# Hybrid decoder layer: the gates' columns in the first v pair, o slots four tiles wide, the mixer's first chunk among the last input slots

## The reference, cut to what matters

```
h    = rms_norm(x) * pre_mix_norm_w                # x: 2048 tokens x 1024
proj = h @ w_in      # columns: q, k (1024), v (512), o (512), gates (8), conv value (512), conv gate (512)
q, k = silu(causal depthwise conv, width 4, of their columns)
i, f = gates + gate_bias                           # 4 heads each
h_tilde = mLSTM(q, k, v, i, log_sigmoid(f))        # 16 chunks of 128 tokens, a state carried on
y_mlstm = sigmoid(o) * head_norm(h_tilde) * mlstm_norm_w
y_conv  = silu(group_norm(causal conv, width 31, of value * sigmoid(gate)))
x = x + rms_norm([y_mlstm, y_conv] @ w_out);  x = x + rms_norm(relu(rms_norm(x) @ w_ff1)^2 @ w_ff2)
```

## Time and profile before

| | |
|---|---|
| time, median of 3 runs | 2147.93 us (2145.79 to 2150.26) |
| the profiled execution | 2149.32 us, of which the span is 2147.5 us |
| PE | 2090.3 us busy, 97% of the span |
| DVE | 1441.8 us, 67% |
| ACT | 903.3 us, 42% |
| mean granted clock of PE | 0.994 of full |

### The profile page before, as it was taken

One profiled execution on the slowest core, in us unless ns is written; L12 is line 12 of the kernel. 1 busy time (PEld: TensorE's weight loads), 2 busy tenths in 40 slices (PEclk: granted clock), 3 DMA queues, 4 the chain that ended last, 5 costly groups with the idle time before them and its releaser, 6 DMA issues. The chain is left out here.

```text
span 2147.5 us, 27070 instructions
## 1 busy us (share of the span) xinstructions
PE 2090.3 (97%) x10177; PEld 1752.4 (82%) x10177; DVE 1441.8 (67%) x1965; ACT 903.3 (42%) x1512; POOL 416.3 (19%) x254
## 2 busy tenths in 40 slices
PE   7999999999979999999999999999999999999998
PEld 5897878888978888778888778888888888888886
DVE  6797999889157777776666866666654536534276
ACT  5532434234344544655544644455423313313153
POOL 0000000000010231243332332233172144400012
PEclk9999999999999999999999999999999999999999
DMA  5021212112174686664455655544875454443375
GB/s 198 25 89 47 67 40 84 55 40 81 55 271 154 223 270 222 210 199 141 139 159 181 227 161 162 162 147 125 280 253 222 142 230 172 175 176 138 137 253 207
DMA packets 253520, 339.18 MB, mean 158 GB/s; under 512 B 11536, under 2 KB 196112, under 8 KB 239568
## 3 DMA queue, kind: packets, MB, share of 16 engines
q1 hardware_dynamic: 219344, 316.29, 43.9%
q10 hardware_dynamic: 33728, 21.04, 3.1%
q0 software_dynamic: 320, 0.13, 0.0%
HBM read 226.14 MB, written 111.28 MB: 157 GB/s over the span
## 5 line engine op out<-in xcount | busy, mean ns | idle before, releaser
L1651 PE MATMUL psum<-x_hi,w_hi_P 128*128 128x512 f32 x896 | 351.6, 392 | 13.1 <-DVE x_lo L1595 8.9
L1855 PE MATMUL psum<-w_hi,hid_hi 128*128 128x512 f32 x896 | 349.3, 390 | 1.9 <-DVE hid_lo L1745 1.9
L1651 PE MATMUL psum<-x_hi,w_lo_P 128*128 128x512 f32 x896 | 350.4, 391 | 0.0
L1651 PE MATMUL psum<-x_lo,w_hi_P 128*128 128x512 f32 x896 | 350.2, 391 | 0.0
L1855 PE MATMUL psum<-w_lo,hid_hi 128*128 128x512 f32 x896 | 349.1, 390 | 0.0
L1855 PE MATMUL psum<-w_hi,hid_lo 128*128 128x512 f32 x896 | 349.1, 390 | 0.0
L1745 DVE TENSOR_TENSOR hid_lo<-hid_raw,hid_hi 128x1024 fp32r<-128x1024 f32 x112 | 182.1, 1663 | 202.4 <-ACT hid_hi L1740 202.4
L1564 POOL TENSOR_TENSOR w_raw<-w_raw 128x512 f32<-128x512 f32 x128 | 179.7, 1427 | 409.6 <-DVE w_lo_P L1577 391.6
L1740 ACT ACTIVATE hid_hi<-hid_raw 128x1024 fp32r<-128x1024 f32 x112 | 112.9, 1051 | 341.5 <-DMA hid_raw<-scratch_hid 341.5
L1577 DVE TENSOR_TENSOR w_lo_P<-w_raw,w_hi_P 128x512 fp32r<-128x512 f32 x224 | 182.4, 826 | 109.1 <-ACT w_hi_P L1573 106.0
L1573 ACT ACTIVATE w_hi_P<-w_raw 128x512 fp32r<-128x512 f32 x224 | 136.7, 627 | 255.0 <-PE psum L1651 254.8
(11 more groups left out here) (241 smaller groups left out, 3895.4 us busy)
## 6 DMA issues: line engine op xcount, KB each, us to landing
scratch_hid<-stage SPq DMA_DIRECT2D x224, 256.0 KB, 3.7
hid_raw<-scratch_hid SPq DMA_DIRECT2D x56, 1024.0 KB, 4.9
w_raw<-in_w SPq DMA_DIRECT2D x52, 1024.0 KB, 5.1
w_grain<-in_w SPq DMA_DIRECT2D x48, 512.0 KB, 4.9
x_raw<-scratch_h2s SPq DMA_DIRECT2D x14, 1024.0 KB, 7.5
w_raw<-in_w_in SPq DMA_DIRECT2D x25, 512.0 KB, 3.6
scratch_h2s<-h2s SPq DMA_DIRECT2D x8, 1280.0 KB, 9.2
scratch_qk<-qout ACTq DMA_DIRECT2D x16, 512.0 KB, 3.1
```

What stands on the lines that cost most here:

```text
L1651: mm = nc.tensor.matmul(psum[:, bank_1(op, g), :], l, r, start=kt == 0 and i == 0, stop=kt == 3 and i == 2)
L1855: mm = nc.tensor.matmul(psum[:, bank, :], l, r, start=f == 0 and k == 0, stop=f == NFP - 1 and k == 2)
```

## The change

- The 8 gate columns move into the weights of the first v pair. A slot of that pair streams 264 columns instead of 256, fills two banks, and begins when the first of its two weight tiles is split. ACT takes the gate columns out to a small tile (`gates`), token by token. PE turns it with two transposes (`gates_t`) after slot 73. The four gates slots, their tile, their stores and their loads go.
- Of the o slots the first six stay as they are (chunks 0 to 5); the other ten (`ow`) have 128 tokens held and four weight tiles streamed: 24 matmuls of 512. The list has 96 slots: o and ow are 80 to 95.
- The gates' row work is cut into four pieces, on DVE at the end of steps 76, 78, 80 and 82 (`forget_rows` to a_max, `carry_rows` to m_in, `floor_rows`, `column_rows`), on PE after slots 76, 78, 79 and 81 (`carry_in`, `carry_out`, `carry_decay`, `columns`), on ACT in steps 74, 78 and 80, each with two table loads.
- Banks go round four from slot 70 on and round two in the last five slots, 91 to 95.
- Chunk 0 runs among these: `scores(0)` after slot 91, `numerators(0)` after 92, `transpose_y(0)` and `scores(1)` after 94, with their work on ACT, DVE and POOL. It has buffers of its own for y.
- The last convolution unit's norm is drawn together (`LAST_UNIT_AT`): sums after slots 88 and 89, the rest in steps 88 and 89. `w_out` is loaded when slot 87 is done, and split in steps 92 to 95.

By the plan's own arithmetic over the new list, the last two convolution units end at steps 79 and 87; `SECOND_TAP` of the last one moves from step 78 to 79. On DVE the splits of tiles o0 and o1 stand in step 75, of o2 in 78, of o3 in 80.

```diff
+O_PAIRS = 3
 SLOTS = (group_slots(0) + pair_slots("v", 0) + group_slots(1) + group_slots(2) + pair_slots("v", 1) + group_slots(3)
-         + [("gates", 0, tb) for tb in range(NTB)] + pair_slots("o", 0) + pair_slots("o", 1))
+         + [("o", pair, m) for pair in range(2) for m in range(O_PAIRS)] + [("ow", 0, c) for c in range(2 * O_PAIRS, NCH)])
...
+RING = [0, 1, 2, 3] + [0, 1] + [2, 3, 0, 1] + [2, 3, 0, 1] + [2, 3] + [0, 1, 2, 3] + [0, 1, 2, 3]
+GATE_COLS = 2 * H
+VG = 2 * P + GATE_COLS
...
+ROWS_SLOT = SLOTS.index(("qk", 6, 0))
+CHUNK_0_SLOT = N_SLOTS - 5
+
+
+def banks_of(s):
+
+    if s >= CHUNK_0_SLOT:
+        return [(s - CHUNK_0_SLOT) % 2]
+    if s >= ROWS_SLOT - 2:
+        return [(s - ROWS_SLOT + 2) % 4]
+    at = s + sum(with_gates(slot) for slot in SLOTS[:s])
+    return [(at + k) % 6 for k in range(2 if with_gates(SLOTS[s]) else 1)]
...
+LAST_UNIT_AT = {AT_MEAN: 1, AT_CENTER: 1, AT_SQUARE: 1, AT_VAR: 2, AT_RSTD: 2, AT_NORM: 2, AT_SILU: 2}
...
-TAIL_SLOT = N_SLOTS - 6
+WO_SPLITS = {CHUNK_0_SLOT + 1: (0,), CHUNK_0_SLOT + 2: (1, 2, 3), CHUNK_0_SLOT + 3: (4,), CHUNK_0_SLOT + 4: (5, 6, 7)}
...
+                first = tile[0] if with_gates(SLOTS[s]) else tile[-1]
+                pe.wait_ge(sem["w_hi"], first + 1)
+                pe.wait_ge(sem["w_lo"], first + 1)
+                for bank in banks:
+                    before = last_in_bank(s, bank)
+                    if before is not None:
+                        by = "dve" if SLOTS[before][0] == "val" else "act"
+                        pe.wait_ge(sem["evac"][by], evacs(before, by))
                 r = RING[tile[0]]
...
+                if with_gates(SLOTS[s]):
+
+                    for k in range(2):
+                        o = psum[:, banks[k], 0:VG]
+                        for kt in range(KT):
+                            if k == 0 and kt == KT // 2:
+                                pe.wait_ge(sem["w_hi"], tile[1] + 1)
+                                pe.wait_ge(sem["w_lo"], tile[1] + 1)
+                            hi, lo = tokens(h_hi, kt, (2 * tb + k) * P, P), tokens(h_lo, kt, (2 * tb + k) * P, P)
+                            pairs = [(hi, vg_hi[:, kt]), (hi, vg_lo[:, kt]), (lo, vg_hi[:, kt])]
+                            for i, (a, b) in enumerate(pairs):
...
+                elif kind == "ow":
+
+                    o = out.rearrange("p (a b) -> p a b", a=W_RING)
+                    for kt in range(KT):
+                        hi, lo = tokens(h_hi, kt, tb * P, P), tokens(h_lo, kt, tb * P, P)
+                        pairs = [(hi, w_hi[:, :, kt, :]), (hi, w_lo[:, :, kt, :]), (lo, w_hi[:, :, kt, :])]
+                        for i, (a, b) in enumerate(pairs):
+                            mm = nc.tensor.matmul(o, a, b, start=kt == 0 and i == 0, stop=kt == KT - 1 and i == 2)
...
-                if s == TAIL_SLOT + 1:
+                if s == ROWS_SLOT + 1:
+                    pe.wait_ge(sem["evac"]["act"], evacs(ROWS_SLOT - 1, "act"))
+                    tail["gates"](pe)
+                if s == ROWS_SLOT + 4:
+                    tail["carry_in"](pe)
+                if s == ROWS_SLOT + 6:
+                    tail["carry_out"](pe)
+                if s == ROWS_SLOT + 7:
+                    tail["carry_decay"](pe)
+                if s == ROWS_SLOT + 9:
+                    tail["columns"](pe)
+                if s == CHUNK_0_SLOT:
                     pe.wait_ge(sem["c_rstd"], 2 * N_UNITS)
-                    tail["carry_in"](pe)
-                if s == TAIL_SLOT + 2:
-                    tail["carry_out"](pe)
-                if s == TAIL_SLOT + 3:
-                    tail["columns"](pe)
+                    scores(0)
+                if s == CHUNK_0_SLOT + 1:
+                    pe.wait_ge(sem["evac"]["act"], evacs(CHUNK_0_SLOT - 1, "act"))
+                    pe.wait_ge(sem["cols_done"], 2)
+                    numerators(0)
+                if s == CHUNK_0_SLOT + 3:
+                    transpose_y(0)
+                    scores(1)
...
+                    both = psum[:, banks[0]:banks[0] + 2, :]
+                    nc.scalar.activation(gates[:, :, :, 2 * tb:2 * tb + 2].rearrange("p g h c -> p c (g h)"),
+                                         both[:, :, 2 * P:VG], ACT.Copy)
+                    ps, to = both[:, :, 0:2 * P], to.rearrange("p (c d) -> p c d", c=2)
...
+                    if u == N_UNITS - 1:
+                        nc.scalar.preload_act_table_set(EXP_TANH)
...
-                if s == TAIL_SLOT:
+                if s == ROWS_SLOT + 2:
                     nc.scalar.preload_act_table_set(LN_EXP)
                     tail["softplus"](act)
                     nc.scalar.preload_act_table_set(SILU_TANH)
-                if s == TAIL_SLOT + 1:
+                if s == ROWS_SLOT + 6:
+                    nc.scalar.preload_act_table_set(LN_EXP)
+                    tail["decay"](act)
+                    nc.scalar.preload_act_table_set(SILU_TANH)
+                if s == ROWS_SLOT + 8:
                     nc.scalar.preload_act_table_set(LN_EXP)
                     tail["exps"](act)
                     nc.scalar.preload_act_table_set(SILU_TANH)
-                if s >= N_SLOTS - 3:
-
-                    if s == N_SLOTS - 1:
-                        nc.scalar.preload_act_table_set(LN_EXP)
-                        tail["weights"](act, 0)
-                    for kt in {N_SLOTS - 3: range(4), N_SLOTS - 2: range(4, 7), N_SLOTS - 1: ()}[s]:
-                        tail["split_wo"](act, kt)
+                if s == CHUNK_0_SLOT:
+                    act.wait_ge(sem["cols_done"], 2)
+                    tail["weights"](act, 0)
+                    first["wk"](0)
+                if s == CHUNK_0_SLOT + 1:
+                    first["yc_high"](0)
+                    nc.scalar.preload_act_table_set(LN_EXP)
+                    first["denominators"](0)
+                    first["head_roots"](0)
+                    nc.scalar.preload_act_table_set(EXP_TANH)
+                if s == CHUNK_0_SLOT + 3:
+                    first["y_high"](0)
+                    tail["weights"](act, 1)
+                    first["wk"](1)
+                for kt in WO_SPLITS.get(s, ()):
+                    tail["split_wo"](act, kt)
+                if s == N_SLOTS - 1:
+                    nc.scalar.preload_act_table_set(LN_EXP)
...
-            tail["rows"](dve)
-            tail["wo_low"](dve, range(KT - 1))
-            tail["exponents"](dve)
+                if s == ROWS_SLOT + 4:
+                    tail["forget_rows"](dve)
+                if s == ROWS_SLOT + 6:
+                    tail["carry_rows"](dve)
+                if s == ROWS_SLOT + 8:
+                    tail["floor_rows"](dve)
+                if s == ROWS_SLOT + 10:
+                    tail["column_rows"](dve)
+                if s == CHUNK_0_SLOT - 1:
+                    first["exponents_0"]()
+                if s == CHUNK_0_SLOT:
+                    first["weigh"](0)
+                if s == CHUNK_0_SLOT + 1:
+                    first["yc_low"](0)
+                    first["update_state"](0)
+                    first["normalise_heads"](0)
+                    first["exponents"](1)
+                if s == CHUNK_0_SLOT + 3:
+                    first["y_low"](0)
+                    first["weigh"](1)
+                tail["wo_low"](dve, WO_SPLITS.get(s, ()))
...
-            sp.wait_ge(sem["proj"], SLOTS.index(("o", 1, NCH // 4 - 1)) + 1)
+            sp.wait_ge(sem["proj"], o_slot(NCH // 2 - 1) + 1)
...
+        def gates_t(pe):
+
+            pe.wait_ge(sem["ident"], 4)
+            for g in range(2):
+                mm = nc.tensor.transpose(psum[0:NG, 4, g * P:(g + 1) * P],
+                                         keep["gates"][:, g].rearrange("p h c -> p (h c)"), ident[:])
+            mm.then_inc(sem["gates_t"], 1)
...
+        def forget_rows(dve):
             nc.vector.memset(state[:], 0.0).then_inc(sem["state"], 1)
             dve.wait_ge(sem["par_b"], 32)
-            dve.wait_ge(sem["ones_a"], 1)
             nc.vector.tensor_scalar(par[:, WO_SCALE:WO_SCALE + H], par[:, WO_SCALE:WO_SCALE + H], 0.5, None,
                                     ALU.mult).then_inc(sem["wo_scale"], 1)
-            dve.wait_ge(sem["gates_in"], 32)
             nc.vector.memset(m_in[:], 0.0).then_inc(sem["m_in"], 1)
-            nc.vector.tensor_scalar(gi[:], gi[:], gate_bias[:, 0:1], None, ALU.add).then_inc(sem["dve_rows"], 1)
-            n_self[0] += 1
             dve.wait_ge(sem["softplus"], 4)
-            link(nc.vector.scalar_tensor_tensor(out=gf[:], in0=gf[:], scalar=0.0, in1=soft[:], op0=ALU.min,
-                                                op1=ALU.subtract))
-            link(nc.vector.tensor_tensor_scan(b_row[:], ones[0:NG], gf[:], 0.0, ALU.mult, ALU.add))
-            link(nc.vector.tensor_tensor(gi[:], gi[:], b_row[:], ALU.subtract))
+            link_row(dve, nc.vector.scalar_tensor_tensor(out=gf[:], in0=gf[:], scalar=0.0, in1=soft[:], op0=ALU.min,
```

(21 more changed lines are left out.)

347 lines of the change are left out of this document (194 added, 153 removed).

## The result

The changed kernel takes 2155.43 us (median of 11 runs, 2151.46 to 2158.89), the kernel before 2148.77 us beside it (11 runs): a ratio of 1.0032, with a 95% interval of 1.0024 to 1.0039. It is 0.3% slower; 2154.0 was forecast. The profiled executions differ by nearly the same: spans of 2153.6 and 2147.5 us, +6.1. Runs of the changed kernel lie up to 7.4 us apart, so that its distance from the forecast, 1.4, is within what one run can shift.

The account below looks back on a forecast made before the run. PE, busy for 97% of the span, was taken as the bound. Work -24.6, first chunk -14.4, old `carry_in` wait -1.4 and new waits +46.5 gave +6.1 us on 2149.3: 2155.4, as median 2154, range 2140 to 2165.

Parts of the forecast that it names:

- Work taken out: PE work that goes or comes with the gates, o and first v pair's slots and `gates_t`: -24.6 us.
- (a): New PE wait at `carry_in` after slot 76, for `a_max` from DVE: +10.5 us, bounds 8.3 and 12.
- (b): New PE wait at `carry_out` after slot 78, for `m_in` from DVE: +6.9 us, bounds 6 and 8.
- (c): New PE wait at `columns` after slot 81, for the exponentials after `floor_rows`: +3.2 us, bounds 0 and 5.
- (d): New PE wait at slot 91, for ACT to take slot 90 out of its bank: +2.2 us, bounds 0.6 and 4.
- (e): New PE wait at `scores(0)` after slot 91, for chunk 0's seven transfers: +8.2 us, bounds 5 and 11.
- its rival: At `scores(0)`: chunk 0's data comes in time, -8.2 and -2.6 us, so 2143 us; chance 0.09.
- (f): New PE wait at `scores(2)`, for chunk 2's loads after the last slot's store: +5.1 us, bounds 3 and 7.
- (g): PE at half clock behind four long waits (`carry_in`, `carry_out`, `scores(0)`, `scores(2)`), 2.6 us each: +10.4 us.
- The first chunk: PE's four waits at the first chunk, 10.8 us, and the half clock with them go: -14.4 us.
- The sum: Whole kernel: -24.6 - 14.4 - 1.4 + 46.5 = +6.1 us, so 2155.4 us profiled and 2154 us as median.
- the row pieces are ready in time: Rival: ACT and DVE run ahead, so PE's waits at `carry_in`, `carry_out` and `columns` vanish: 2128 us; chance 0.12.

Follow-up runs that it names:

- e9_late_rows: Changed kernel with chunk 0's work put back behind slot 95 and the row work two slots later: 2125.8 us.
- e1_rows: Changed kernel with the tail's row work on PE, and the ACT and DVE steps moved with it, two slots later: 2130.2 us.
- e3_bank: Changed kernel with the two banks of the output slots from slot 91 on swapped: 2156.9 us.
- e2_loads: Changed kernel with the loads of chunks 0 and 1 issued in the order in which their data is ready, y_c last: 2147.6 us.
- e7_all_chunk2: Changed kernel with row work two slots later, loads of chunks 0 and 1 reordered, last slots' banks swapped, chunk 2's loads ahead of the next stage's weights: 2120.6 us.
- e4_fill: Changed kernel with 96 unused matmuls on PE ahead of `carry_in`, `carry_out` and `scores(0)`: 2151.1 us.
- e10_late_all: Changed kernel with row work later, loads reordered, banks swapped, chunk 2's loads ahead, y_c counted apart, but chunk 0 behind slot 95: 2123.6 us.
- e11_o_narrow: Changed kernel with row work later, loads reordered, banks swapped, chunk 2's loads ahead, y_c counted apart, and all sixteen o slots two tiles wide: 2143.8 us.

## Why the prediction was right

- **Work taken out**, -24.6: measured 25.2 in the last column of the table; e9_late_rows, which keeps it and little else, is 25.5 under the kernel before. One size inside it was off: the first v pair's slots are 5.80 apart (157.02 - 151.22), not 5.9, against 5.76 before. Eight columns more cost 0.04 us a slot, 0.3 for the eight, the lower end of its bounds. The earlier begin of the first of these slots gave back a wait: 1.7 us before, at 115 us, and 0.4 after. At 300 us the changed kernel was 0.9 ahead (299.33 against 300.23 for the same evacuation), within the -1.5 to +1.3 given, of which the sum took 0.
- **(a) to (c)**, +10.5, +6.9, +3.2 (its terms give 7.0 and 3.3 for the last two): measured 10.5, 6.6 and 3.0, on the releasers named. Slot 87's end was forecast 29 us later and is 28.8 later. e1_rows shows them to be the price of the places: with PE's part two slots later all three are gone. That (b) "starts from slot 77, so (a) doesn't hide it" is seen in the 14.02 us for which ACT idles. No wait for DVE's taps was put down, and none is there; in e1_rows, where PE isn't held up, one of 1.4 us for `c_buf` shows at 498 us, which the standing had covered.
- **(d)**, +2.2: 1.9. e3_bank shows that it was not a cost of its own: it lay before (e), and (e) would have been 10.3 without it. In the sum the two were rightly worked out one behind the other.
- **(e)**, +8.2: 8.3, on the load of the broadcast row. e2_loads shows that 6.2 of it were the queue's order and conditions; the prediction's grounds against its rival (the loads can't be issued before the store lands) hold for the list as written, and by what the data needs for y_c alone.
- **(f)**, +5.1: 4.9, shown to be the loads by e7_all_chunk2.
- **(g)**, +10.4: 2.6, 2.5, 2.8 and 1.4, so 9.3. The wait of 3.0 at `columns` brought 1.7 more that was not counted (529 to 537 us, in steps of 1 us), so that the sum is near 11. That the two errors nearly cancel is luck. The step behind the miss is "longer than the 4.8 us after which it fell": the clock fell behind shorter waits too. That standing brings it, e4_fill shows for `carry_out` and `scores(0)`.
- **The first chunk**, -14.4, and from slot 87 to the second half of chunk 0's projection some 22 us less: 23.8 less. e10_late_all shows the 13.8 us that the interleaving removes; with what then stands at `scores(2)` and chunk 1 it is worth 9.7.
- **The sum**: waits and clock were forecast at -14.4 - 1.4 + 46.5 = +30.7, and the traces have +31.0 between 440 and 760 us. The mechanisms are right one by one; that the total agrees to 1.4 us is in part luck, as single terms were off by up to 1.7.
- **Not foreseen**: what the o slots' order does to the load of `w_out`. It changed nothing in the sum, because the rows of the new list already had the load at slot 87, but who takes 3.2 us for the whole worth of the four-tile slots is 26 us off where chunk 0 is interleaved (e11_o_narrow).

Of the rivals, "the row pieces are ready in time" would have been 2128 and is what e1_rows reached, at 2130.2, by giving them two slots. It was right about the price and wrong about the place.

## What to carry to other kernels

Work moved forward into a busy list costs at the place where the engines that feed it stand, not where its own operations are short: read what is ahead of it on each of them, and give it the slots that this takes. Here two slots turned a loss of 0.3% into a gain of 0.9%. Before loads are blamed for being late, look at the queue's order, at what each really has to wait for, and at what their counter counts together: a piece needed last should neither stand ahead of nor be counted with the pieces needed first. A wait in front of a longer one is free, and becomes the next one to pay for when the longer goes.
